# Feed-forward weight sums of a two-block model: one 128x1024 add per round on GpSimd instead of VectorE

## The reference

```
def swiglu(h, w_in, w_out):
    gate, up = jnp.split(h @ w_in, 2, axis=-1)
    return (jax.nn.silu(gate) * up) @ w_out
```

## Time and profile before

| what | value |
|---|---|
| median of 3 runs | 3531.89 us (3523.72 to 3532.7) |
| the profiled execution's own time | 3528.36 us |
| its span, first to last instruction | 3526.5 us |
| TensorE matmul busy | 3337.7 us (95%) |
| VectorE busy | 2334.9 us (66%) |
| ScalarE busy | 1581.9 us (45%) |
| GpSimd busy | 482.5 us (14%) |
| mean granted TensorE clock | 0.975 |

### The profile page before, as it was taken

The page is one execution under the profiler, slowest core; times in us unless marked ns, Lnnn a source line. Parts: engine busy times, 40 slices in busy tenths (PEclk is TensorE's granted clock), DMA queues, the critical chain, the costliest instruction groups (busy, mean ns, idle before and its releaser), DMA issues. The chain is left out here.

```text
span 3526.5 us, 59587 instructions
## 1 busy us (share of the span) xinstructions
PE 3337.7 (95%) x24514; PEld 2835.4 (80%) x24514; DVE 2334.9 (66%) x3196; ACT 1581.9 (45%) x2553; POOL 482.5 (14%) x399
## 2 busy tenths in 40 slices
PE   8999999899999899999998999999999989889998
PEld 8998676778998699886767789986899856659986
DVE  7877476448875588754744488755887258658852
ACT  5552435236552455524352365524655253645541
POOL 0003113540003000031125300030000100310001
PEclk9999999999999999999999999999999999999999
DMA  4235211012235223452100122342333222122331
GB/s 157 100 131 186 73 60 38 3 49 96 103 132 160 72 108 108 137 162 73 65 26 4 49 96 103 135 158 73 126 108 106 86 68 72 44 82 85 108 104 64
DMA packets 81589, 327.38 MB, mean 93 GB/s; under 512 B 11904, under 2 KB 11904, under 8 KB 65832
## 3 DMA queue, kind: packets, MB, share of 16 engines
q1 hardware_dynamic: 81320, 323.57, 26.9%
HBM read 321.15 MB, written 4.74 MB: 92 GB/s over the span
## 5 line engine op out<-in xcount | busy, mean ns | idle before, releaser
L235 DVE TENSOR_TENSOR w_low<-w_raw,w_high 128x1024 fp32r<-128x1024 f32 (+1 forms) x241 | 340.2, 1412 | 466.0 <-ACT w_high L227 465.1
L227 ACT ACTIVATE w_high<-w_raw 128x1024 fp32r<-128x1024 f32 (+1 forms) x241 | 284.5, 1182 | 538.0 <-PE ffa_ps L253 172.5
L833 DVE TENSOR_TENSOR w_low<-w_raw,w_high 128x1024 fp32r<-128x1024 f32 (+1 forms) x186 | 220.9, 1187 | 21.4 <-ACT w_high L712 10.7
L712 ACT ACTIVATE w_high<-w_raw 128x1024 fp32r<-128x1024 f32 (+1 forms) x186 | 190.2, 1023 | 3.0 <-PE ffa_ps L253 1.6
L251 PE MATMUL mix_proj_ps<-mix_x_high,w_high 128*128 128x512 f32 x416 | 171.8, 413 | 12.2 <-DVE mix_x_low L400 12.0
L253 PE MATMUL mix_proj_ps<-mix_x_high,w_low 128*128 128x512 f32 x416 | 167.4, 402 | 0.0
L252 PE MATMUL mix_proj_ps<-mix_x_low,w_high 128*128 128x512 f32 x416 | 166.4, 400 | 0.0
L251 PE MATMUL ffa_ps<-ffa_hid_high,w_high 128*128 128x512 f32 x352 | 141.7, 402 | 1.7 <-DVE w_low L235 1.7
L251 PE MATMUL b_f_ps<-b_f_hid_high,w_high 128*128 128x512 f32 x352 | 139.3, 396 | 1.7 <-DVE w_low L235 1.7
L252 PE MATMUL b_f_ps<-b_f_hid_low,w_high 128*128 128x512 f32 x352 | 139.0, 395 | 0.0
L253 PE MATMUL b_f_ps<-b_f_hid_high,w_low 128*128 128x512 f32 x352 | 138.9, 395 | 0.0
(11 more groups left out here) (739 smaller groups left out, 10978.0 us busy)
## 6 DMA issues: line engine op xcount, KB each, us to landing
ffa_quarters<-in_ffa_seven SPq DMA_DIRECT2D x40, 1024.0 KB, 4.8
ffb_quarters<-in_ffb_seven SPq DMA_DIRECT2D x40, 1024.0 KB, 4.8
b_f_quarters<-in_ffn_seven SPq DMA_DIRECT2D x40, 1024.0 KB, 4.9
w_raw<-in_mix_in SPq DMA_DIRECT2D x77, 512.0 KB, 3.4
w_raw<-in_ffa_out SPq DMA_DIRECT2D x32, 704.0 KB, 5.4
w_raw<-in_ffb_out SPq DMA_DIRECT2D x32, 704.0 KB, 5.3
w_raw<-in_ffn_out SPq DMA_DIRECT2D x32, 704.0 KB, 4.1
ffa_ada_raw<-in_w_ada SPq DMA_DIRECT2D x80, 256.0 KB, 2.8
```

Source lines behind the costliest of these rows:

```text
L227: act.activation(self.high[:, self.place(n, 0, kt)], self.raw[:, n % SLOTS, :kt * P], ACT.Copy).then_inc(self.rounded, 1)
L235: dve.tensor_tensor(self.low[:, whole], self.raw[:, n % SLOTS, :kt * P], self.high[:, whole].bitcast(F32), ALU.subtract).then_inc(self.spl ...
L712: act.activation(ops.split(group, r)[0], ops.source(group, r), ACT.Copy).then_inc(part_rounded, 1)
L833: dve.tensor_tensor(low, ops.source(group, r), high.bitcast(F32), ALU.subtract).then_inc(part_split, 1)
```

## The change

GpSimd makes s13, with a semaphore `ends_made` of its own. VectorE's `add_ends` is gone from all its places; `add_second` waits for `ends_made`, and so does ScalarE's rounding of g3. `SUMS` counts the two sums that are left.

```diff
-SUMS = numbers([("s13", 0), ("s2", 0)]
-               + [(n, r + ahead) for r in range(SEVEN) for n, ahead in (("s13", 1), ("s4", 0), ("s2", 1)) if r + ahead < SEVEN])
+SUMS = numbers([("s2", 0)] + [(n, r + ahead) for r in range(SEVEN) for n, ahead in (("s4", 0), ("s2", 1)) if r + ahead < SEVEN])
...
             @block.gpsimd
             def _(pool):
                 halves.gpsimd(pool)
+                both = lambda ap: ap.rearrange("p (a c) -> p a c", a=2)
+                for r in range(SEVEN):
+                    pool.wait_ge(landed[r % RAWS], 16 * (r // RAWS + 1))
+                    if r == 0:
+                        pool.wait_ge(ws.split, out0)
+                    else:
+                        pool.wait_ge(part_split, SPLITS["g3", r - 1])
+                        pool.wait_ge(sum_made, SUMS["s2", r - 1])
+                    pool.tensor_tensor(both(ops.s13), repeat(ops.part(r, 3, 4), 1, 2), both(ops.part(r, 0, 2)), ALU.add)\
+                        .then_inc(ends_made, 1)
                 finish.gpsimd(pool)
...
-                act.wait_ge(sum_made, SUMS["s13", 0])
+                act.wait_ge(ends_made, 1)
                 round_part("g3", 0)
...
-                        act.wait_ge(sum_made, SUMS["s13", r + 1])
+                        act.wait_ge(ends_made, r + 2)
...
-                def add_ends(r):
-                    dve.wait_ge(landed[r % RAWS], 16 * (r // RAWS + 1))
+                def add_second(r):
+                    dve.wait_ge(ends_made, r + 1)
                     if r > 0:
-                        dve.wait_ge(part_split, SPLITS["g3", r - 1])
-                        dve.wait_ge(sum_made, SUMS["s2", r - 1])
-                    both = lambda ap: ap.rearrange("p (a c) -> p a c", a=2)
-                    dve.tensor_tensor(both(ops.s13), repeat(ops.part(r, 3, 4), 1, 2), both(ops.part(r, 0, 2)), ALU.add)\
-                        .then_inc(sum_made, 1)
-
-                def add_second(r):
-                    dve.wait_ge(sum_made, SUMS["s4", r - 1] if r > 0 else SUMS["s13", r])
+                        dve.wait_ge(sum_made, SUMS["s4", r - 1])
...
-                add_ends(0)
                 split_part("g1", 0)
...
-                    if r + 1 < SEVEN:
-                        add_ends(r + 1)
```

More of the change, by code:

```diff
@@ L642, in feed_forward @@
         names = ["gated", "multiplied", "hid_rounded", "hid_ready", "small_landed", "taken", "t_made", "t_rounded", "t_ready",
-                 "product_done", "sum_made", "part_rounded", "part_split", "copied", "silu_first", "silu_second", "combined"]
+                 "product_done", "sum_made", "ends_made", "part_rounded", "part_split", "copied", "silu_first", "silu_second", "combined"]
         with stage(nc, name, [*names, *landed_names, *halves.names, *finish.names, *(n for part in beside for n in part.names)]) as (block, *sems):
-            (gated, multiplied, hid_rounded, hid_ready, small_landed, taken, t_made, t_rounded, t_ready, product_done, sum_made,
+            (gated, multiplied, hid_rounded, hid_ready, small_landed, taken, t_made, t_rounded, t_ready, product_done, sum_made, ends_made,
              part_rounded, part_split, copied, silu_first, silu_second, combined) = sems[:len(names)]
```

## The result

The changed kernel takes 3572.7 us (3569.8 to 3573.7, 4 runs), the kernel before 3529.7 in the same runs: a ratio of 1.0124 (95% interval 1.011 to 1.0138), 43 us slower. The span grew from 3526.5 to 3571.9 us.

A forecast was written before the change was run, and what follows sets the result against it. TensorE was taken to bound steady rounds, with VectorE 1.8 us ahead, and VectorE the openings. Openings 17.4 plus b_f rounds 6.5 gave 23.9 us on 3528.4, so 3552.3, stated as 3554; forecast 3541 to 3580, wide range 3529 to 3592.

The forecast's parts named there:

- The block: Steady rounds: g2's split, two SBUF operands, waits for GpSimd's whole add and ends 1.09 us after it; PSUM readers untouched.
- The loop: c22 to c22 through VectorE: 10.06 us; nothing lost in ffa and ffb, 0.19 us a round in b_f, 6.5 us.
- The opening: Start of each feed forward: three GpSimd adds make the first c22 2.9 us later, 17.4 us over six.
- the upper bound: Whole kernel with a GpSimd add of 2.58 us: loop 10.28, drift 31 us, openings 21 us, giving 3580 us.
- The first rival (no blocking): GpSimd's adds block VectorE hardly or only where there is slack, not slower: 3522 to 3532 us; chance 0.22.
- the wide range: Whole kernel: 3529 to 3592 us, holding the forecast, the first rival's upper part and the second's lower part.
- The second rival: Rounds: blocking more than once, g2's split first or a late landing; half a us a round, 3597 us; chance 0.15.
- what was to be seen in the changed trace: g2's split about 3.2 us, b_f spacing 10.06, add 2.36, first c22 about 49.3, TensorE's c22 waits some 30.
- a sign of more blocking than counted: Steady ffa rounds: waits of TensorE there would show the forecast wrong; no size given.

The follow-up runs named there:

- the late run: Changed kernel, GpSimd's add also waiting for the multiplication of gate and up two rounds back (opening's last work in rounds 1, 2): 3541.9 us, ratio 1.0033.
- The two runs with a fill and a copy: Changed kernel, GpSimd's add replaced by a constant fill of s13: 3522.5 us, ratio 0.9979; by a copy of two quarters: 3524.9 us, ratio 0.999.
- The run without GpSimd's work: Kernel before the change, with t4's split done four times in place of once: 3559.1 us, ratio 1.0085.

## Why the prediction was right in its mechanism and short in its size

**The block** was the step that carried the case, and it held to the hundredth: an instruction of VectorE with two SBUF operands ends 1.08 us after GpSimd's add (1.09 forecast), one that reads PSUM is untouched (0.42 us under the add of the late run). GpSimd gets in first, as forecast, in all steady rounds but one. The two runs with a fill and a copy show the cause.

**The loop** was forecast at 10.06 us and measured 10.16. Both missing parts are GpSimd's own: its wake-up took 0.13 us, not 0.08, and its add 2.41, not the 2.36 of the nearest row. The sum set the loop against TensorE's 10.03 (10.05 by the spacing of c22) and found next to nothing to pay in ffa and ffb. Where two loops are as close as this, 0.10 us is the whole price: over 17 rounds and six feed forwards it is 10 us. Forecast for the steady rounds 6.5 us, measured 16.4.

**The opening** was forecast at 2.9 us late, measured 3.2 to 3.4; 17.4 us against 19.8. It holds three adds, and each brings some 0.1 us more of wake-up and length.

**The clock** was not in the sum. I had TensorE standing idle for 4 us in each opening and priced the stall alone. Behind it the granted clock was 0.50 for 3.4 or 6.8 us and took another 10 us over six openings. The run without GpSimd's work shows that it is the stall that brings it.

Together 23.9 + 10 + 10 + 2 = 46 against a measured span of 45.4 more. That the time of 3572.7 us lies in the forecast's 3541 to 3580 is partly luck: the upper bound was worked out with an add of 2.58 us, which did not happen, and the room that this left was filled by the clock, which no bound held.

The first rival (no blocking) is refuted, and the part of the wide range below 3541 was there for its sake. The second rival, with half a us a round, did not happen as a cost, but the order that it feared is there once, in the first b_f:

```profile
2640.61 1.22 DVE L835 TENSOR_TENSOR w_low<-w_raw,w_high 128x1024 fp32r<-128x1024 f32 x1
2641.74 2.88 DVE L835 TENSOR_TENSOR b_f_last<-b_f_quarters,b_f_last 128x512 fp32r<-128x512 f32 x1
```
```profile
2640.78 3.30 POOL L668 TENSOR_TENSOR w_raw<-b_f_quarters 128x1024 f32<-128x1024 f32 x1 [8.04 <-DVE w_low L835]
```

GpSimd started 0.42 us after g3's split in place of 0.13 (its transfer had landed 1.2 us before; why it was late is open). g2's split got in first, the add waited for it and held up g4's split. L894 came only 0.04 us later for it: the turn moved the block by one instruction and did not add a second. Two rounds of b_f lasted 10.48 and 10.43 us, this one and another in the usual order, and in both the 0.3 us lie between the end of L894 and ScalarE's copy, 0.37 us in place of 0.09. No run shows why.

Of what was to be seen in the changed trace, GpSimd's add beginning right behind g3's split, g2's split above 3.2 us and the first c22 at about 49.3 us (49.19) came out; TensorE's waits for c22 are 27.2 us for a forecast 30. Waits in ffa's steady rounds were named as a sign of more blocking than counted. They are there, 0.11 us a round at the start of s4, too short for the list of waits, and they come from a longer add and wake-up, not from a second block.

## What to carry to other kernels

Before work goes from VectorE to GpSimd, look at what VectorE will run while GpSimd reads SBUF. If it is an instruction with two SBUF operands, VectorE pays what is left of GpSimd's instruction (2.13 us of its 2.41 here) to be rid of its own 1.14. Put GpSimd's work where VectorE waits, reads PSUM or has time to spare: the adds of rounds 3 to 19 cost 22 us behind g3's split and nothing behind the multiplication. And a place where TensorE already waits is the dearest place for delay, since it is paid in full and TensorE's clock may fall behind it. A wait list that shows nothing does not show that nothing is paid: compare the spacing of rounds as well.

## What the runs showed that I had not expected

- A single pass that held both VectorE's own add and the block used up 1.54 us of VectorE's lead of 1.7. A lead of this kind covers one late pass and not a lasting lag.
- In openings of a kernel otherwise busy on TensorE, the clock stood at 0.50 for 3.4 or 6.8 us behind each of the 18 stalls of 3.7 to 5.0 us and behind five of six of 2.6 us; after waits of up to 1.83 us it stayed at 1.00.
- GpSimd's fill of 128x1024 took 0.95 us and its copy 1.04, both shorter than VectorE's add of that size, while its add took 2.41.
